# Expert weights of a mixture layer: gate and up loaded in 8 KB runs, their splits queued behind the SiLUs and the row copies, high halves multiplied first, row numbers fetched one turn ahead

## The reference

```python
grp = argmax(h @ w_rg + b_rg)                 # 1 of 4 groups
top_v, top_i = lax.top_k(le_sel, TOP_K)       # 2 of the group's 8 experts
xb  = h_pad[tok]                              # 128 sorted rows of one expert
hid = jax.nn.silu(xb @ w_gate[e]) * (xb @ w_up[e])   # (1024 -> 512), twice
out = hid @ w_down[e]                         # (512 -> 1024)
out = jnp.zeros(...).at[slot_tok].add(yb * slot_w)   # weighted, summed by token
```

## Time and profile before

| | |
|---|---|
| time, median of 3 runs | 2329.09 us (2324.69 to 2329.18) |
| profiled execution, its own time | 2325.89 us |
| its span in the trace | 2324.2 us |
| PE / DVE / ACT / POOL busy | 94% / 60% / 45% / 27% |
| first gate product to last down product of the experts | about 1380 to 2269 us |

### The profile page before, as it was taken

One profiled execution on the slowest core, in us unless ns is written; L12 is line 12 of the kernel. 1 busy time (PEld: TensorE's weight loads), 2 busy tenths in 40 slices (PEclk: granted clock), 3 DMA queues, 4 the chain that ended last, 5 costly groups with the idle time before them and its releaser, 6 DMA issues.

```text
span 2324.2 us, 35398 instructions
## 1 busy us (share of the span) xinstructions
PE 2175.7 (94%) x11618; PEld 1833.7 (79%) x11619; DVE 1401.4 (60%) x2033; ACT 1055.0 (45%) x1518; POOL 636.4 (27%) x648
## 2 busy tenths in 40 slices
PE   8999999999999669999999979999999999999890
PEld 5888888899999558888788858778788888887770
DVE  6322222377555568888566665765767675647876
ACT  4422332243222126565333234755666665547763
POOL 0000000000000558887222232331333323223333
PEclk9999999999999989999999989999999999999995
DMA  8632333546552987666554335998988888868998
GB/s 310 241 106 110 127 136 146 185 156 218 171 162 71 326 323 260 213 222 220 172 218 146 118 125 171 344 284 256 339 267 267 268 272 257 241 173 273 349 348 327
DMA packets 297276, 518.10 MB, mean 223 GB/s; under 512 B 33332, under 2 KB 205948, under 8 KB 292424
## 3 DMA queue, kind: packets, MB, share of 16 engines
q1 hardware_dynamic: 270840, 439.52, 55.2%
q0 software_dynamic: 17136, 43.92, 8.5%
q10 hardware_dynamic: 9216, 33.56, 3.6%
HBM read 397.28 MB, written 128.57 MB: 226 GB/s over the span
## 4 chain that ended last, share of the span: by engine, by line
PE 45%; DMA 7%; issue 4%; DVE 4%; POOL 2%; ACT 1%; POOLq 0%; SPq 0%; DVEq 0%; ACTq 0%
PE r_py L2559 8%; PE r_py L2061 8%; PE r_py L2554 6%; PE r_py L2550 6%; PE r_py L2551 6%; DMA e_w_whole<-in_moe_w_up_dram 3%; DMA e_x<-second_norm,e_ids 3%; PE m_bank L1687 2%; DMA e_ids<-tokens_sorted 1%; DVE e_w_low L2656 1%; PE r_pT L2531 1%; PE m_bank L1653 1%; PE r_pl L2070 1%; PE m_bank L1619 1%; PE m_bank L1667 1%
## 5 line engine op out<-in xcount | busy, mean ns | idle before, releaser
L2656 DVE TENSOR_TENSOR e_w_low<-e_w_whole,e_w_high 128x2048 fp32r<-128x2048 f32 x192 | 431.1, 2287 | 90.9 <-ACT e_w_high L2610 84.5
L2610 ACT ACTIVATE e_w_high<-e_w_whole 128x2048 fp32r<-128x2048 f32 x190 | 353.9, 1915 | 28.8 <-DMA e_w_whole<-in_moe_w_down_dram 16.5
L2550 PE MATMUL r_py<-e_w_high,e_xT 128*128 128x512 f32 x768 | 300.2, 391 | 1.2 <-ACT e_xT L2603 1.2
L2551 PE MATMUL r_py<-e_w_low,e_xT 128*128 128x512 f32 x768 | 300.0, 391 | 0.0
L897 PE MATMUL proj_acc<-w_high,hT_high 128*128 128x512 f32 x672 | 263.9, 393 | 0.1
L897 PE MATMUL proj_acc<-w_low,hT_high 128*128 128x512 f32 x672 | 262.0, 390 | 0.0
L897 PE MATMUL proj_acc<-w_high,hT_low 128*128 128x512 f32 x672 | 261.7, 389 | 0.0
L2559 PE MATMUL r_py<-e_w_high,e_hT 128*128 128x512 f32 x768 | 226.1, 406 | 17.4 <-ACT e_hT L2622 17.3
L2554 PE MATMUL r_py<-e_w_high,e_xT 128*128 128x512 f32 x768 | 189.9, 389 | 0.0
L2559 PEld LDWEIGHTS r_py<-e_w_high,e_hT 128*128 128x128 f32 x768 | 138.7, 191 | 45.1 <-ACT e_hT L2622 20.0
L2550 PEld LDWEIGHTS r_py<-e_w_high,e_xT 128*128 128x128 f32 x768 | 145.0, 189 | 31.8 <-issue 1.6
(11 more groups left out here) (314 smaller groups left out, 4180.3 us busy)
## 6 DMA issues: line engine op xcount, KB each, us to landing
e_w_whole<-in_moe_w_gate_dram SPq DMA_DIRECT2D x64, 1024.0 KB, 9.7
e_w_whole<-in_moe_w_up_dram SPq DMA_DIRECT2D x64, 1024.0 KB, 12.3
e_w_whole<-in_moe_w_down_dram SPq DMA_DIRECT2D x64, 1024.0 KB
by_token<-tok SPq DMA_DIRECT2D x32, 512.0 KB, 3.0
w_in_raw<-in_w_mod_dram SPq DMA_DIRECT2D x32, 512.0 KB, 6.0
m_tok<-by_token SPq DMA_DIRECT2D x16, 768.0 KB, 5.4
s_kv<-by_token SPq DMA_DIRECT2D x20, 512.0 KB, 5.6
modulated_high<-hT_high SPq DMA_DIRECT2D x9, 1024.0 KB, 3.9
```

What stands on the lines that cost most here:

```text
L2550: nc.tensor.matmul(pG[:, half], xT[:, 0, k], wh[:, half, w], start=(k == 0), stop=False)
L2551: nc.tensor.matmul(pG[:, half], xT[:, 0, k], wl[:, half, w], start=False, stop=False)
L2610: nc.scalar.activation(wh[:, third, part], raw[:, third, part], ACT.Copy).then_inc(whs.sem, 1)
L2656: nc.vector.tensor_tensor(wl[:, third, part], raw[:, third, part], wh[:, third, part].bitcast(F32), ALU.subtract).then_inc(wls.sem, 1)
```

## The change

Five things change, all but a few lines of them in `experts`.

- **Layout.** Partition p now holds rows 8p to 8p+7 of gate and up. Third 0 is the first four of them with all 512 columns, third 1 the other four, so each of the two transfers of a third reads and writes 8 KB runs. The channels of the normed rows `h2` are permuted to match: one operation of `residual` (`h2m`) writes with a stride of 128 floats, the additive row of the modulation is permuted once, and the router's weights are read in the same order.
- **Split order.** `low(following, 0)` and `high(following, 0)` leave their place between the two halves of the hidden rows and stand behind the small splits, directly ahead of third 1.
- **Product order.** PE starts with the high part of third 0 on both column halves, then the low rows, then the low weights of third 0, then third 1. Both column halves need both thirds.
- **Row numbers.** `held` has five slots; the load goes straight into slot 4 and is waited for one turn later. `take`, the buffer `ids` and its waits are gone.
- **Start.** Block 0's rows are gathered in POOL's first turn, behind the first shift and the first scatter, and no longer in `residual`. DVE clears `y` before, and waits for the second load of row numbers before it makes its first piece.

```diff
+def sixth_of(buf, third, n, whole):
+    if third == 2 or whole:
+        part = buf[:, third, n * THIRD // 2:(n + 1) * THIRD // 2]
+        return part.rearrange("p (j f) -> p j f", f=256) if third < 2 else part
+    return buf[:, third].rearrange("p (j n f) -> p j n f", n=2, f=256)[:, :, n]
...
     if third < 2:
-        to = raw[:, third].rearrange("p (k n f) -> p k n f", k=KD, n=2)[:, :, n]
-        eng.dma_start(to, io[src][0, bass.ds(e, 1), :, third * 256:(third + 1) * 256].rearrange("o (k p) f -> p (o k) f", p=P)).then_inc(landed, 16)
+        rows = KD // 2
+        to = raw[:, third, n * THIRD // 2:(n + 1) * THIRD // 2].rearrange("p (k f) -> p k f", k=rows)
+        eng.dma_start(to, io[src][0, bass.ds(e, 1)].rearrange("o (p k) f -> p (o k) f", k=KD)[:, third * rows:(third + 1) * rows]).then_inc(landed, 16)
...
-            for half in range(2):
-                pe.wait_ge(hids.sem, hids.at(b - 1, half + 1))
-                pe.wait_ge(xTs.sem, xTs.at(b))
-                pe.wait_ge(wls.sem, wls.at(expert_of[0], 2 * half + 2))
-                for k in range(KD):
-                    w = slice(k * 512, (k + 1) * 512)
-                    nc.tensor.matmul(pG[:, half], xT[:, 0, k], wh[:, half, w], start=(k == 0), stop=False)
-                    nc.tensor.matmul(pG[:, half], xT[:, 0, k], wl[:, half, w], start=False, stop=False)
-                pe.wait_ge(xTl.sem, xTl.at(b))
-                for k in range(KD):
-                    m = nc.tensor.matmul(pG[:, half], xT[:, 1, k], wh[:, half, k * 512:(k + 1) * 512], start=False, stop=(k == KD - 1))
-                m.then_inc(prodG.sem, 1)
+            pe.wait_ge(xTs.sem, xTs.at(b))
+            pe.wait_ge(whs.sem, whs.at(expert_of[0], 2))
+            for half in range(2):
+                pe.wait_ge(hids.sem, hids.at(b - 1, half + 1))
+                gate_up(half, 0, wh, 0)
+            pe.wait_ge(xTl.sem, xTl.at(b))
+            for half in range(2):
+                gate_up(half, 1, wh, 0)
+            pe.wait_ge(wls.sem, wls.at(expert_of[0], 2))
+            for half in range(2):
+                gate_up(half, 0, wl, 0)
+            pe.wait_ge(whs.sem, whs.at(expert_of[0], 4))
+            for half in range(2):
+                gate_up(half, 0, wh, 1)
+                gate_up(half, 1, wh, 1)
+                pe.wait_ge(wls.sem, wls.at(expert_of[0], 4))
+                gate_up(half, 0, wl, 1).then_inc(prodG.sem, 1)
...
                 nc.vector.scalar_tensor_tensor(out=hid[:, half * 256:(half + 1) * 256], in0=sg[:, half], scalar=held[:, 1, 2:3].bitcast(F32), in1=pG[:, half, 1], op0=ALU.mult, op1=ALU.mult).then_inc(hids.sem, 1)
-                if following is not None and half == 0:
-                    low(following, 0)
...
             if following is not None:
+                low(following, 0)
                 low(following, 1)
...
-        dve.wait_ge(g["ids_issued"].sem, g["ids_issued"].at(0))
+        nc.vector.memset(y[:], 0.0).then_inc(none.sem, 1)
+        dve.wait_ge(ids_in.sem(0), ids_in.at(1))
         low(0, 0)
-        nc.vector.memset(y[:], 0.0).then_inc(none.sem, 1)
...
+        def turn(c, row, following):
+            shift(c)
             row = row + P if following is None else following * STRIDE
-            pool.dma_start(ids[:], dram["ids"][bass.ds(row, P), :]).then_inc(ids_in.sem(0), 16)
-            scatter(b)
-            pool.wait_ge(ids_in.sem(0), ids_in.at(b))
+            pool.dma_start(held[:, 4], dram["ids"][bass.ds(row, P), :]).then_inc(ids_in.sem(0), 16)
+            scatter(c)
+            gather(c)
+            landed(c)
+            rows_landed(c)
```

More of the change, by code:

```diff
@@ L2497, in load @@
+        pool.wait_ge(none.sem, none.at(0))
+        count = over_blocks(pool, turn)
+        c = pool.snap(count, min_val=0, max_val=2 * NE)
+        shift(c)
+        scatter(c)
+        gather(c)
+        landed(c)
+        rows_landed(c)
+        for n in (1, 2):
+            pool.wait_ge(hids.sem, hids.at(c + (n - 3)))
             pool.sem_inc(junk.sem, 1)
-            gather(b)
-            landed(b)
-            pool.wait_ge(x_in.sem(0), x_in.at(b))
+            nc.gpsimd.tensor_copy(held[:, 0:4 - n], held[:, 1:5 - n]).then_inc(held_on.sem, 1)
+            pool.wait_ge(held_on.sem, held_on.at(c + n))
@@ L2603, in xT_copy, with high_sixth @@
             nc.scalar.activation(xT[:, 0], pX[:], ACT.Copy).then_inc(xTs.sem, 1)
+        def high_sixth(third, n):
+            nc.scalar.activation(sixth_of(wh, third, n, False), sixth_of(raw, third, n, True), ACT.Copy).then_inc(whs.sem, 1)
         def high(e, third):
@@ L2608, in high @@
             for n in range(2):
-                part = slice(n * HALF, (n + 1) * HALF)
-                nc.scalar.activation(wh[:, third, part], raw[:, third, part], ACT.Copy).then_inc(whs.sem, 1)
+                high_sixth(third, n)
         def body(b, row, following):
```

111 lines of the change are left out of this document (48 added, 63 removed).

## The result

| | before | after |
|---|---|---|
| median | 2326.89 us (4 runs, 2324.40 to 2329.18) | 2375.6 us (4 runs, 2373.70 to 2379.07) |
| ratio, 95% interval | | 1.021 (1.0196 to 1.0223) |
| profiled execution, span | 2324.2 us | 2371.8 us |
| first gate product | 1379.95 | 1384.07 |
| first turn | 23.34 us | 25.82 us |

The change makes the kernel 2.1% slower, 2375.6 us where 2368 were forecast. The 95% interval of the ratio keeps well clear of 1. The last two rows are distances between the first gate products of turns; the last turn ends with its last down product. At 17.706 us each the 47 turns would take 832.2 us, so 33.4 us were lost in them before and 74.6 us after.

The account below looks back on a forecast made before the run. PE, busy 94% of the span, was taken to set the pace, with 33.3 us lost to stalls. Queue +71.6, transfers -33.3 and start +2.3 gave +40.6 us; the forecast was 2368 us, range 2346 to 2386.

Parts of the forecast that it names:

- The DVE queue: Expert turns: six pieces and the copy precede the next hidden half; PE waits 2.31 us per new expert, +71.6 us.
- the wait for ACT's high part: Start of a new expert's turn: PE waits 0.55 us for ACT's first pair, inside the 2.31 us.
- The transfers: Expert stage: 8 KB runs remove all DMA stalls, -33.3 us; slow turns would need between 17.6 and 20.8 us.
- the DMA share in these turns: Sign: in runs of one-block experts the DMA share would be near 0.9.
- Row numbers: POOL's turns: the wait for the numbers leaves the turn, taken as 0 us.
- The start: Block 0's gather issues 5.4 us later; the next step comes 2.3 us later, bounds 0 and +5.4.
- 7 us to land: First turn: second gather issued some 3 us after PE's start, landing 7 us later, moved by POOL about 1395.5.
- The first product: Sign: PE's first expert product would come near 1385 us.
- The strided write: Permuted rows in `residual`: 0.6 us a tile, 9 us for 16 unhidden; taken as 0, bounds 0 and +9.
- the 2 us that would have been a sign of being wrong: Sign of error: `residual` ending more than 2 us late.
- The sum: Whole kernel: 71.6 - 33.3 + 2.3 = +40.6 us, giving 2369.7 us as median; 2368 us was forecast.
- faster: Rival, chance 0.12: DVE's queue does not push the hidden rows back, only transfers count, 2296 us.

Follow-up runs that it names:

- Version 7: Changed kernel with one of third 0's two pieces (high and low) moved behind the first SiLU and hidden half, each sixth loaded by itself: 2308.95 us.
- version 12: Version 7 with both loads of a third issued together behind both its low pieces: 2317.18 us.
- version 3: Changed kernel with gate, up and down loads cut in two, gate and up in 1 KB runs, four transfers a third: 2383.71 us.
- version 4: Kernel before with only the new row number handling and the new start; layout, split and product order as before: 2326.19 us.
- version 6: Changed kernel with SP's loads of expert 1 held back until the rows of block 1 have landed: 2371.55 us.
- version 5: Kernel before with only the splits of third 0 moved behind the small splits: 2456.25 us.

## Why the prediction came out as it did

- **The DVE queue: right, in place and size.** Forecast 2.31 us for each new expert, 71.6 in all; the 47 turns lost 74.6 us, 2.41 each. Of them 1.4 are the wait for hidden half 0 and 0.5 the wait for ACT's high part at the turn's start, as foretold; the rest is that PE's own rows behind a wait are longer (18.10 and 17.86 busy in the windows instead of 17.70 twice, 0.56 us). Version 7, which takes one piece out of the queue, removes it, so it is shown and not only argued. It also loads by sixths; version 12, which loads by thirds as the changed kernel does, still takes 62.1 of the 74.6 us away.
- **The transfers: the sum right, and largely hidden.** The stalls of 33.3 us went, and the one-block turns came to 20.17 us in the mean, forecast 20.02. That a slow turn would need "between 17.6 and 20.8, nearer the first" is borne out by version 7 (17.89) and by the last turns there (18.8 at 390 GB/s, where nothing is left that was loaded early). After the change most of it is not seen, because 20.02 us of DVE stand above it: going back to 1 KB in version 3 cost 13.2 us in the 47 turns, not 33. One sign missed: the DMA share in these turns was to be near 0.9, and it was 0.99 to 1.02. The 33.3 us were also not all waits for transfers. PE's waits in the 47 turns before come to 22.3 us (17.4 for the transposed hidden rows, 4.9 for the second half), and in three slow turns the granted clock fell to 0.50 behind a wait of 1.9 to 2.1 us, though three others of 2.0 to 2.1 us left it at 1.00. The first of them, 21.42 us where the slow turns at full clock take 19.7 to 20.9:

```profile
1642.96:1664.38 21.42, 19.55 (x86) 15.88 (x84) 17.05 (x13) 15.36 (x14) 6.43 (x5) 0.92 1.07 343
```

In the changed kernel the clock stays at 1.00 in all 47 turns, where PE waits 1.2 to 1.8 us for the hidden rows. Three turns at a mean clock of 0.92 are some 5 of the 33.3 us.
- **Row numbers: right,** 0 taken, and none measured (version 4).
- **The start: mis-sized,** +2.3 us forecast, +6.6 between the two profiled executions (first product +4.1, first turn +2.5), beyond the upper bound of 5.4. The step that failed is "7 us to land" for the second gather. It was issued 2.8 us after PE's start, as counted, and took 12.9 us, so PE waited 4.27 us and transposed the first hidden rows 4.9 us later than before, where 2.3 were forecast. I had counted the longer runs only as a gain; version 6, which keeps them away from the gather, prices that at 4.05 us. But with 1 KB runs it would not have been 7 us either (9.8 and 10.5 in versions 4 and 3); that much the products nearly cover, PE waits 0.2 and 1.25 us. The other 1.7 us are the lower clock behind PE's wait, which the sum didn't have.
- **The first product: near 1385 by luck.** It came at 1384.07, with another split than forecast. From the last DMA that writes `tokens_sorted` to the first product the kernel before takes 15.1 us (version 5, which has the same start, 15.3) and the changed kernel 17.5 (version 4: 17.6). So the new start costs some 2.4 us and not 5.4. The other 1.8 us arise ahead of it, in `residual`.
- **The strided write: the bound was too low in size, and 0 was right in effect.** I took at most 0.6 us a tile; it takes 0.80 (2073 - 1276), 12.8 us in 16 tiles. PE hides nearly all of it, as assumed. From the end of the last product of `residual` (L2061 before) to that last DMA it is 24.8, 24.8 and 25.3 us in the three kernels without the permuted rows and 25.6 to 26.1 in the eleven with them, so they cost 0.2 to 1.3 us there, less than the 2 us that would have been a sign of being wrong. The 0.56 ns an element came from a reduction beside an addition, two different operations, so it was a weak ground for a bound. Advanced Engine Details and Errata, SBUF Cachelines, in the Trainium skill announces a penalty for such accesses; there is one, and it is less than the doubling I put beside it.
- **The sum.** 74.6 - 33.4 + 6.6 = 47.8 us, and the spans differ by 47.6; forecast were 71.6 - 33.3 + 2.3 = 40.6. The 7 us between are 3.0 of the queue and 4.3 of the start. The 2368 us that were forecast lie 1.7 us under the 2369.7 that the prediction's own sum gave.

Of the rivals, "faster" had its decision point at 1.0 us of wait per expert. Version 7 is that case: by leaving 8 us of loss in all 47 turns it reaches 2309, where that rival gave 2296. It took a first piece one place earlier, which the change does not do.

Not settled: why executions scatter by up to 5 us ahead of the experts. The last product of `residual` ends at 1340.02 us before, at 1342.65 in version 5, which is the same kernel up to there, and between 1340.50 and 1344.71 in those with the permuted rows. Most of the scatter of the first product is there already. Neither the product order nor the new layout was tested alone.

## What to carry to other kernels

Work that fills an in-order engine to 92% of a turn (DVE here, 16.5 of 17.9 us) can't be moved in blocks: count the pieces between one deadline and the next, and move one at a time. If a faster transfer shows little gain, look for the queue that has just become the longer one before giving up the transfer: with the queue set right the change comes to -0.2% in 1 KB runs and to -0.8% in 8 KB runs, instead of +2.1%. A short transfer beside longer runs lands later: hold a prefetch back while something small and urgent is under way, and stop lengthening runs where the rate no longer rises. A DMA share near 1 doesn't show that the transfers are the limit.
